# Weight pieces split into high and low parts whole: one operation of 128x2048 on each engine and one wait of TensorE for a piece

## The reference

```python
for l in range(2):                       # first block, two layers
    q, k, v, gu, gv = split(rms_norm(x) @ w_in[l])       # 2048 x 3584
    x = x + concat(attention(q, k, v), gating(gu, gv)) @ w_o[l]
    a = conv(rms_norm(x) @ w_up[l])                      # 2048 x 11264
    g, u = split(a)
    x = x + (silu(g) * u) @ w_down[l]                    # 5632 x 2048
mod = silu(c) @ w_ada + b_ada            # second block: 2048 x 12288, one or two rows
... hl @ w_in_2, mixers, @ w_out_2
x = x + g2 * (relu(hl2 @ w_mlp1_2) ** 2 @ w_mlp2_2)
return rmsnorm(x, final_norm_w_2)
```

## Time and profile before

| what | value |
|---|---|
| median of 3 runs | 3447.2 us (3446.84 to 3450.77) |
| profiled execution, its own time | 3450.32 us |
| its span, first to last instruction | 3448.5 us |
| mean granted TensorE clock | 0.993 |
| TensorE busy | 3383.4 us, 98% |
| VectorE busy | 2414.6 us, 70% |
| ScalarE busy | 1617.3 us, 47% |
| DMA, weights queue | 63.8% of 16 engines, 202 GB/s over the span |

### The profile page before, as it was taken

How to read it: one execution, slowest core, us unless ns; L and a number is a source line. 1 busy time by engine, 2 the same in 40 slices (tenths; PEclk the granted TensorE clock), 3 DMA queues, 4 the chain that set the end, 5 groups by cost and what they waited for, 6 DMA issues and landing times.

```text
span 3448.5 us, 43214 instructions
## 1 busy us (share of the span) xinstructions
PE 3383.4 (98%) x16110; PEld 2800.2 (81%) x16110; DVE 2414.6 (70%) x3087; ACT 1617.3 (47%) x2165; POOL 33.9 (1%) x29
## 2 busy tenths in 40 slices
PE   8999999999999999999999999999989999999998
PEld 7888888888888888888888887778866788888887
DVE  6667888888666666777787676666776675757576
ACT  6645555555344645555555444234443444334343
POOL 0000000000000000000000000000000000000000
PEclk9999999999999999999999999999999999999999
DMA  7557777777677557777777773346614566666675
GB/s 263 157 177 222 226 222 227 230 221 233 227 250 217 155 179 223 232 219 232 232 232 247 266 241 110 107 139 185 211 58 138 167 217 206 212 205 218 200 225 165
DMA packets 369476, 697.80 MB, mean 202 GB/s; under 512 B 25487, under 2 KB 37792, under 8 KB 368672
## 3 DMA queue, kind: packets, MB, share of 16 engines
q1 hardware_dynamic: 368736, 694.91, 63.8%
q10 hardware_dynamic: 576, 0.62, 0.1%
HBM read 689.15 MB, written 6.29 MB: 202 GB/s over the span
## 4 chain that ended last, share of the span: by engine, by line
PE 89%; DVE 5%; DMA 1%; DVEq 1%; ACT 1%; issue 1%; ACTq 0%; POOL 0%; SPq 0%; POOLq 0%
PE acc L2255 17%; PE acc L2257 17%; PE acc L2256 17%; PE acc L2543 6%; PE acc L2545 6%; PE acc L2544 6%; PE acc L2561 3%; PE acc L2562 2%; PE side L2561 2%; PE turn L2561 2%; DVE w_lo L1363 1%; DMA w_raw<-in_w_down 1%; PE turn L2465 1%; PE turn L2276 1%; PE side L2562 1%; PE turn L2562 1%
## 5 line engine op out<-in xcount | busy, mean ns | idle before, releaser
L1363 DVE TENSOR_TENSOR w_lo<-w_raw,w_hi 128x1024 fp32r<-128x1024 f32 x708 | 837.8, 1222 | 366.4 <-ACT w_hi L848 333.5
L848 ACT ACTIVATE w_hi<-w_raw 128x1024 fp32r<-128x1024 f32 x708 | 738.9, 1061 | 699.2 <-DMA w_raw<-in_w_up 321.3
L2255 PE MATMUL acc<-w_hi,in_hl 128*128 128x512 f32 x1408 | 552.5, 392 | 0.0
L2257 PE MATMUL acc<-w_hi,in_hl 128*128 128x512 f32 x1408 | 548.5, 390 | 0.0
L2256 PE MATMUL acc<-w_lo,in_hl 128*128 128x512 f32 x1408 | 548.1, 389 | 0.0
L1322 ACT ACTIVATE w_hi<-w_raw 128x1024 fp32r<-128x1024 f32 x252 | 266.3, 1060 | 374.5 <-DMA w_raw<-in_w_mlp 373.8
L2169 DVE TENSOR_TENSOR w_lo<-w_raw,w_hi 128x1024 fp32r<-128x1024 f32 x252 | 301.6, 1222 | 169.6 <-ACT w_hi L1322 160.7
L1468 DVE SCALAR_TENSOR_TENSOR ada_sum<-w_raw,silu_c,ada_sum 128x512 f32<-128x512 f32 x450 | 327.6, 750 | 30.5 <-issue 6.1
L2255 PEld LDWEIGHTS acc<-w_hi,in_hl 128*128 128x128 f32 x1408 | 264.4, 188 | 55.7 <-issue 1.3
L2257 PEld LDWEIGHTS acc<-w_hi,in_hl 128*128 128x128 f32 x1408 | 264.2, 188 | 55.3
L2256 PEld LDWEIGHTS acc<-w_lo,in_hl 128*128 128x128 f32 x1408 | 264.5, 188 | 53.4
(11 more groups left out here) (413 smaller groups left out, 5555.4 us busy)
## 6 DMA issues: line engine op xcount, KB each, us to landing
w_raw<-in_w_up SPq DMA_DIRECT2D x352, 512.0 KB, 3.8
w_raw<-in_w_mlp SPq DMA_DIRECT2D x256, 512.0 KB, 3.9
w_raw<-in_w_in SPq DMA_DIRECT2D x200, 512.0 KB, 3.7
w_raw<-in_w_ada SPq DMA_DIRECT2D x192, 512.0 KB, 4.2
w_raw<-in_w_down SPq DMA_DIRECT2D x176, 512.0 KB, 4.7
w_raw<-in_w_o SPq DMA_DIRECT2D x64, 512.0 KB, 3.8
w_raw<-in_w_out SPq DMA_DIRECT2D x32, 512.0 KB, 3.8
K<-k_store SPq DMA_DIRECT2D x16, 256.0 KB, 6.9
```

Of the source, the lines that this page charges most:

```text
L848: nc.scalar.activation(hi[s][:, ks], raw[s][:, ks], ACT.Copy).then_inc(w_hi[s][h], 1)
L1363: nc.vector.tensor_tensor(lo[s][:, ks], raw[s][:, ks], hi[s][:, ks].bitcast(F32), ALU.subtract).then_inc(w_lo[s][h], 1)
L2255: nc.tensor.matmul(acc[p][i][:], high(kt)[:, tok], hi[s][:, k], start=(kt == first), stop=False)
L2257: last = nc.tensor.matmul(acc[p][i][:], low(kt)[:, tok], hi[s][:, k], start=False, stop=(kt == final))
```

## The change

All operations that split a piece are made whole. ScalarE waits for both halves of the load, makes one copy of 128x2048 and raises only `w_hi[s][1]`. VectorE waits for that, makes one subtraction of 128x2048 and raises only `w_lo[s][1]`. TensorE waits for `w_lo[s][1]` once, before its first matmul on the piece. Loads stay in halves, and so does the freeing of the slots. One small piece of the second block (`FIRST[DT]`, 32 columns) keeps its two operations, behind one wait. `ada_half` is not changed.

```diff
@@ ScalarE
         def split_hi(s, r, n=4):
             for h in range(2):
-                ks = slice(2 * h, min(2 * h + 2, n))
                 act_.wait_ge(w_loaded[s][h], r * 16)
-                nc.scalar.activation(hi[s][:, ks], raw[s][:, ks], ACT.Copy).then_inc(w_hi[s][h], 1)
+            nc.scalar.activation(hi[s][:], raw[s][:], ACT.Copy).then_inc(w_hi[s][1], 1)
@@ the hidden stage's split on ScalarE
                         act_.wait_ge(w_loaded[s][h], r * 16)
-                        nc.scalar.activation(hi[s][:, 2 * h:2 * h + 2], raw[s][:, 2 * h:2 * h + 2], ACT.Copy).then_inc(w_hi[s][h], 1)
+                    nc.scalar.activation(hi[s][:], raw[s][:], ACT.Copy).then_inc(w_hi[s][1], 1)
@@ VectorE
         def split_lo(s, r, n=4):
-            for h in range(2):
-                ks = slice(2 * h, min(2 * h + 2, n))
-                dve.wait_ge(w_hi[s][h], r)
-                nc.vector.tensor_tensor(lo[s][:, ks], raw[s][:, ks], hi[s][:, ks].bitcast(F32), ALU.subtract).then_inc(w_lo[s][h], 1)
+            dve.wait_ge(w_hi[s][1], r)
+            nc.vector.tensor_tensor(lo[s][:], raw[s][:], hi[s][:].bitcast(F32), ALU.subtract).then_inc(w_lo[s][1], 1)
@@ TensorE, product
             for k in range(4):
                 kt = k0 + k
-                if k % 2 == 0:
-                    pe.wait_ge(w_lo[s][k // 2], r)
+                if k == 0:
+                    pe.wait_ge(w_lo[s][1], r)
```

More of the change, by code:

```diff
@@ L1146, in split_hi2 @@
                 act_.wait_ge(w_loaded[s][h], r * 16)
-                v = (lambda w: dt_view(w, h)) if n == FIRST[DT] else lambda w: w[:, 2 * h:2 * h + 2]
-                nc.scalar.activation(v(hi[s]), v(raw[s]), ACT.Copy).then_inc(w_hi[s][h], 1)
+                if n == FIRST[DT]:
+                    nc.scalar.activation(dt_view(hi[s], h), dt_view(raw[s], h), ACT.Copy).then_inc(w_hi[s][h], 1)
+            if n != FIRST[DT]:
+                nc.scalar.activation(hi[s][:], raw[s][:], ACT.Copy).then_inc(w_hi[s][1], 1)
         def square_sum2(src, dst):
@@ L1801, in split_lo2 @@
             s, r = ring(n)
+            dve.wait_ge(w_hi[s][1], r)
             for h in range(2):
-                dve.wait_ge(w_hi[s][h], r)
-                v = (lambda w: dt_view(w, h)) if n == FIRST[DT] else lambda w: w[:, 2 * h:2 * h + 2]
-                nc.vector.tensor_tensor(v(lo[s]), v(raw[s]), v(hi[s]).bitcast(F32), ALU.subtract).then_inc(w_lo[s][h], 1)
+                if n == FIRST[DT]:
+                    nc.vector.tensor_tensor(dt_view(lo[s], h), dt_view(raw[s], h), dt_view(hi[s], h).bitcast(F32), ALU.subtract).then_inc(w_lo[s][h], 1)
+            if n != FIRST[DT]:
+                nc.vector.tensor_tensor(lo[s][:], raw[s][:], hi[s][:].bitcast(F32), ALU.subtract).then_inc(w_lo[s][1], 1)
         def diagonal(r):
@@ L2534, in product2 @@
             for h in range(2):
-                pe.wait_ge(w_lo[s][h], r)
+                if h == 0:
+                    pe.wait_ge(w_lo[s][1], r)
                 wh, wl = hi[s][:, 2 * h:2 * h + 2], lo[s][:, 2 * h:2 * h + 2]
```

## The result

The changed kernel takes 3521.5 us (median of four executions, 3519.9 to 3528.1) against 3449.0 us for the kernel before (3446.8 to 3451.3). The ratio is 1.0212, with a 95% interval of 1.0199 to 1.0224: slower by 72.5 us. The forecast was slower by 46, at 3493 us in a range of 3465 to 3522. The direction and the mechanism held; the size was forecast too small by 26.5 us. The time lies in rival B's region (above 3512), at the range's very end.

A forecast was written before the change was run, and what follows sets the result against it. TensorE's stream was taken as the bound, so added idle time is the cost. Terms 1.9 + 1.7 + 8.4 + 13 + 7 + 3.7 + 1.7 + 5.6 + 3 gave 46.0 us, hence 3493 us, range 3465 to 3522.

The forecast's parts named there:

- rival B: Down stages: every slot that VectorE frees is late; 3537 us, or 3515 with half that excess; chance 0.12 (above 3512).
- (1): Start: the first piece's low part is ready at 18.33 against a TensorE start of 16.46; +1.9 us.
- (2): Gating, once in each layer: the low part ahead of the gated rows ends 0.85 us later, twice; +1.7 us.
- (3): Up stages: low parts in VectorE's order behind a turned block make TensorE wait, up to 1.07 each; +8.4 us (6.4 to 25).
- (4): First layer's down stage: late splits delay modulation sums, freed slots and next loads, so lateness accumulates; +13 us (bounds 4.5, 39).
- (5): Second layer's down stage: same order with sums half as long, taken as half the first layer's; +7 us (1.5 to 20).
- (6): End of second down stage: four splits chained with the context's rows, +3.7 us; two more before the first filter, +1.7.
- (8): Clock: two losses from TensorE running at half speed after stalls of near 3 us; +3 us (0 to 8).
- (7): Second block: low parts ending VectorE's chain behind a convolution and at like or smaller places; +5.6 us (3 to 8).
- A: Down stages: the ring absorbs lateness, each stage costs its one largest lateness, no long stalls; 3476 us, chance 0.22.
- C: VectorE's chains between turned block and product: saved fixed parts make the kernel faster, 3409 us; chance 0.04.
- D: No difference: second halves are ready in spite of the order; 3440 to 3454 us, chance 0.04.

The follow-up runs named there:

- rest_whole: Against the kernel before: every piece whole with one TensorE wait, except those of the two down stages, which keep halves; 3477.4 us, ratio 1.0079.
- act_whole: Against the kernel before: only ScalarE's operation whole; VectorE still subtracts two halves and TensorE waits for each half; 3507.5 us, ratio 1.0166.
- wait_one: Against the kernel before: only TensorE changed, waiting for both low halves before a piece's first matmul; ScalarE and VectorE keep halves; 3470.8 us, ratio 1.0061.
- dn1_whole: Against the kernel before: whole pieces and one TensorE wait in the second layer's down stage alone; 3483.0 us, ratio 1.0090; repeated, 3482.5 us.
- whole_ada_first: Changed kernel (everything whole) with VectorE's modulation sum ahead of the split in the down stages; 3485.0 us, ratio 1.0101 to the kernel before.

## Why the prediction was right in direction and too small

*What bounds the kernel, and the large operations.* Right. VectorE's operation took 2292 ns as taken, ScalarE's 1918 ns where I took 1.95 us with bounds of 1.85 and 2.01. The Trainium skill ("ScalarE: Activation LUTs", What ACT_TABLE_LOAD costs) makes it an estimate of 1.89 us; the row lies between the two.

*(1) Start*, +1.9: the two profiles show +1.0 (17.43 against 16.46). The experiments with halves at the start begin at 15.6 to 15.8 us, rest_whole at 17.8, which is near 2. So the term was up to 0.9 too large. *(2), (3) Gating and up stages*, 10.1 together, less the start, which lies ahead of the table: its first and third rows give 8.1 + 3.2 = 11.3. Right, and for the most part at the very places; two waits for the attention's scores (0.54 and 0.85 us) I had not named, and (2)'s difference is 0.82 us, not 0.85. Changed kernel, timeline of TensorE:

```profile
404.96 0.50 PE L2254 MATMUL acc<-w_hi,in_hl 128*128 128x512 f32 x1 [0.89 <-DVE w_lo L1362]
```

act_whole and wait_one show whose price it is: TensorE's wait, behind VectorE's order.

*(4) First down stage*, +13: the loop is the one that I walked through. I had three stalls, of 2.9, 2.7 and 2.9 us; they came as 3.39 us (901.83, one piece before its forecast place), 2.27 (924.21) and 3.01 (938.40). Low was the 4.5 us for the two column chunks behind them, where I took the ring to have more slack: the stalls there are 3.60, 0.93 and 2.94 us. The stage's idle part is 16.6 us, so the term was a little low.

*(5) Second down stage*, +7: the step that failed. "I take half of (4)", because its sums are half as long and TensorE hardly waited there. With (6) I had 10.7; the idle part alone is 20.3 and the stage 31.5 us longer. Up to the context's chain TensorE was idle for 0.4 us in the kernel before (to 2060.47) and for 19.1 us in the changed one (to 2122.89, the last 1.5 of them a wait of that chain). So the term measures some 17.6 us: as much as the first stage's 16.6, not half of it. The number of waits in the kernel before says how often the ring ran dry, not how far it was from that; and SyncE's wait for VectorE there (37.0 us in 16 waits, against 67.4 in 20) would have spoken for half as well. A third piece of work stands in VectorE's order there, the low part of the activations. Changed kernel, timeline of VectorE:

```profile
1905.28 2.29 DVE L1362 TENSOR_TENSOR w_lo<-w_raw,w_hi 128x2048 fp32r<-128x2048 f32 x1 [2.86 <-ACT w_hi L847]
1907.67 1.58 DVE L1467 SCALAR_TENSOR_TENSOR ada_sum<-w_raw,silu_c,ada_sum 128x512 f32<-128x512 f32 x2
1909.48 1.23 DVE L1732 TENSOR_TENSOR al<-act,ah 128x1024 fp32r<-128x1024 f32 x1 [0.23 <-issue]
1910.66 2.29 DVE L1362 TENSOR_TENSOR w_lo<-w_raw,w_hi 128x2048 fp32r<-128x2048 f32 x1
```

From one split to the next it is 5.38 us, against 5.44 of TensorE's for a piece: once late, VectorE hardly catches up. That this makes up for the shorter sums is argued from the rows, not tried; that it loses by itself was shown (dn1_whole).

*(8) Clock*, +3: the other step that failed, and the larger one in the profiled execution. The mean granted clock is 0.993 over 3448.5 us before and 0.987 over 3526.3 after: 24.1 and 45.8 us of full clock lost, a difference of 21.7 (TensorE's busy time grew by 24.4 us over the stages, not all of it clock). I had two losses of 1.7 us; in the down stages alone six stalls are followed by the lower level. whole_ada_first, with stalls of at most 1.5 us in the down stages but for the one that ends the second, has 0.6 and 0.7 us of extra busy time there, against 5.2 and 11.2. Without the clock my terms make 43 us. Of the 32 us that were missing in this execution's span, some 19 are the clock; 13 were lost beside it, 9 of them as added idle time.

The execution with the profile is the slowest of the four, and the clock is why it misleads a little: the other three had 0.990, 0.991 and 0.990 over some 3519 us, which is 32 to 35 us of full clock lost, 8 to 11 more than before (an estimate, with 2 us of rounding in each figure). So of the 72.5 us between the medians about 10 are the clock, and most of what the forecast lacks there, near 20 of 26.5 us, is what TensorE loses at full clock. Where it loses that, only the profiled execution shows: there (5) was low by 10.6 us and (4) by 3.6, and what the other terms had too much takes 5 of it back.

*(6)*, the four splits in the context's chain, forecast 3.7, came to about 3.1 from 2060.47 (2122.89) to the chain's end, 1.6 of it busy time, and 1.2 more at its first wait. *(7) and the second block's two filter splits*, 7.3 together: 12.6 in the table, 6.7 of it busy time, so the idle part (5.9) was near. *Hidden stages*, 0: −1.2. Right.

*Rivals.* A (the ring absorbs the down stages) and D are out. C, faster: the saving in fixed parts is real, 43.9 us of VectorE's and 87.0 of ScalarE's busy time, and the time rises all the same. The Trainium skill's rule ("VectorE: DVE Perf Modes", The TRN2 errata) that one large tile pays the latency once agrees with the busy time; it says nothing of when the first half is done, and that decided. B had the size and half of the account: the sign that I had named for it, SyncE waiting much longer for VectorE, came (92.9 us for 67.4, 68.6 for 37.0), but its price did not: not every slot was late by 1.95 us (25.5 us over 23 waits is 1.1 each), and the first stage's idle part is 16.6 us, not 39.

## What to carry to other kernels

Merging two pipelined halves into one operation saves its fixed part and delays the first result by half an operation on each engine that it passes; on this kernel, bound by another engine, only the delay counted. Look for a loop through the buffers: where an engine frees a slot in program order behind an operation that itself waits for a load, a delay of 1 or 2 us comes round again and grows, and put the freeing work ahead of the waiting work: here that gave back 36.5 of the 72.5 us with whole operations, and 3 us with halves. Do not halve a term because the kernel before hardly waits there. Price a stall of TensorE of 3 us with the stretch at the lower clock that can follow it (some 1.6 us for the one worked out above; six of eight such stalls in the down stages were followed by one), and compare the granted clock of the profiled execution with that of the others before its share is taken for the kernel's.

## What was not expected of the hardware

- The clock's share: 21.7 us of 77.8 in the profiled execution, with the same 16110 matmuls, and only about half as much in the other three.
- A stall of 3.60 us left the granted clock at 1.00, while one of 2.80 us in the same kernel was followed by the lower level. The length of a stall alone does not tell.
- Loads held back by a slot came at 393 GB/s once it was free, against a mean of 198 GB/s: at these stalls the loads lacked a free slot, not bandwidth.
- Two stalls of TensorE of up to 4.6 us with nothing to wait for, in a stage whose splits were left as before, at the same two matmuls in two runs of one program; the kernel before and the changed one lose 0.5 to 0.7 us at each.
